# Three feed-forwards of a two-layer hybrid trunk: six leading weight tiles per half instead of four

## The reference, cut to what matters

```python
def swiglu(h, wg, wu, wd):
    return (jax.nn.silu(h @ wg) * (h @ wu)) @ wd

def sandwich_in(h, m, sub, p):
    return rms_norm(h, p['norm_pre'][sub]) * (1 + m[:, 3 * sub + 1]) + m[:, 3 * sub]

def sandwich_out(h, y, m, sub, p, weight):
    return h + weight * m[:, 3 * sub + 2] * rms_norm(y, p['norm_post'][sub])

def ffn_sub(h, m, sub, j, p):
    y = swiglu(sandwich_in(h, m, sub, p), p['w_gate'][j], p['w_up'][j], p['w_down'][j])
    return sandwich_out(h, y, m, sub, p, 0.5)

mod_x = (jax.nn.silu(c) @ w_mod[l] + b_mod[l]).reshape(bsz, N_MOD, 1, d)   # and mod_c from c_ctx
```

## Time and profile before

| | us |
|---|---|
| median of 3 runs | 2919.39 (2917.44 to 2920.51) |
| profiled execution | 2921.65 |
| its span, first to last instruction | 2919.8 |
| mean granted TensorE clock | 0.979 |

### The profile page before, as it was taken

One profiled execution on the slowest core, in us unless ns is written; L12 is line 12 of the kernel. 1 busy time (PEld: TensorE's weight loads), 2 busy tenths in 40 slices (PEclk: granted clock), 3 DMA queues, 4 the chain that ended last, 5 costly groups with the idle time before them and its releaser, 6 DMA issues.

```text
span 2919.8 us, 44695 instructions
## 1 busy us (share of the span) xinstructions
PE 2775.6 (95%) x17096; PEld 2649.4 (91%) x17096; DVE 2024.1 (69%) x3481; ACT 1095.6 (38%) x1888; POOL 805.3 (28%) x619
## 2 busy tenths in 40 slices
PE   6999999999999889999999899999999998899998
PEld 5999999988878889999999899999978877899997
DVE  4877889657345768989886789889656447664334
ACT  3312324453443452324245233324444534522233
POOL 2700313240043275312225821313240123400002
...
GB/s 231 136 154 134 128 130 94 144 149 56 89 55 33 109 152 76 128 137 91 136 100 144 134 113 102 131 129 87 152 133 58 127 36 81 133 144 89 93 93 111
DMA packets 468063, 332.24 MB, mean 114 GB/s; under 512 B 36118, under 2 KB 419452, under 8 KB 467340
## 3 DMA queue, kind: packets, MB, share of 16 engines
...
## 4 chain that ended last, share of the span: by engine, by line
PE 73%; DVE 12%; POOL 4%; ACT 4%; issue 4%; DMA 1%; SPq 0%; POOLq 0%; ACTq 0%; DVEq 0%
PE ps L2282 21%; PE ps L2284 21%; PE ps L2283 21%; POOL scr L842 3%; ACT wsp L1061 2%; DVE wsp L1581 2%; DVE macc L1624 2%; PE ps L2710 2%; PE ps L2685 1%; PE ps L2686 1%; DVE hn L1687 1%; POOL wsp L851 1%; ACT hn L1112 1%; PE ps L2697 1%; PE ps L2344 1%
## 5 line engine op out<-in xcount | busy, mean ns | idle before, releaser
L2282 PE MATMUL ps<-hn,wsp 128*128 128x384 f32 (+1 forms) x2400 | 785.7, 327 | 38.4 <-DVE hn L1687 19.3
L2283 PE MATMUL ps<-hn,wsp 128*128 128x384 f32 (+1 forms) x2400 | 776.3, 323 | 0.0
L2284 PE MATMUL ps<-hn,wsp 128*128 128x384 f32 (+1 forms) x2400 | 775.9, 323 | 0.0
L1581 DVE TENSOR_TENSOR wsp<-raw,wsp 128x1024 fp32r<-128x1024 f32 (+2 forms) x304 | 349.7, 1150 | 325.0 <-ACT wsp L1061 323.4
L2282 PEld LDWEIGHTS ps<-hn,wsp 128*128 128x128 f32 x2400 | 459.9, 192 | 56.8 <-issue 23.3
L1061 ACT ACTIVATE wsp<-raw 128x1024 fp32r<-128x1024 f32 (+2 forms) x344 | 324.9, 945 | 470.8 <-PE ps L2284 255.4
L2283 PEld LDWEIGHTS ps<-hn,wsp 128*128 128x128 f32 x2400 | 461.0, 192 | 0.0
L2284 PEld LDWEIGHTS ps<-hn,wsp 128*128 128x128 f32 x2400 | 460.4, 192 | 0.0
L2282 PE MATMUL ps<-aT,wsp 128*128 128x384 f32 (+1 forms) x1344 | 439.8, 327 | 16.6 <-DVE wsp L1581 5.6
L2284 PE MATMUL ps<-aT,wsp 128*128 128x384 f32 (+1 forms) x1344 | 433.7, 323 | 0.0
L2283 PE MATMUL ps<-aT,wsp 128*128 128x384 f32 (+1 forms) x1344 | 433.7, 323 | 0.0
(11 more groups left out here) (288 smaller groups left out, 4847.2 us busy)
## 6 DMA issues: line engine op xcount, KB each, us to landing
...
raw<-in_ffn_w_down SPq DMA_DIRECT2D x128, 192.0 KB, 2.8
...
```

The lines of the kernel that those rows point to most:

```text
L1581: dve.tensor_tensor(wsp[:, t % 2, 1, 0:width], raw[:, t % RAW, 0:width], wsp[:, t % 2, 0, 0:width].bitcast(F32), ALU.subtract).then_inc(wl ...
L2282: pe.matmul(dst, w(0), x(0), start=first, stop=False)
L2283: pe.matmul(dst, w(0), x(1), start=False, stop=False)
L2284: return pe.matmul(dst, w(1), x(0), start=False, stop=last)
```

## The change

In the three feed-forwards after the first:

- The lead has three chunks, six tiles, per half (`head_chunks`, `LONG_BANKS`): tiles 0 to 5 on half 0 and 6 to 11 on half 1. One whole chunk and the half chunk are left in group 0. Matmuls are as many as before; two more tiles are loaded and split in each.
- The mean for half 1 stands in the fifth tile, (4, 3), its spreading ahead of the sixth, (5, 0). GpSimd makes the low parts of tiles 2, 6 and 7 (before: 2 and 5).
- Tiles 4 and 5 take PSUM banks 1 and 3, so the scaled slices of half 1 go to SBUF, into `wsum` (`tmpS`, `scaled`).
- The splits of tiles 8 to 11 stand between the activations of the lead.
- Group 0's gate and up phase has no modulation; its eight pieces go to down tiles: in (0,1) and (1,0) four more in group 0's down phase, two each at the last down tile of groups 1 and 2; in (1,1) eight at down tiles 2 to 5 of group 0.

```diff
+def head_chunks(l, j): return 2 if (l, j) == (0, 0) else 3
+def up_tiles(l, j, g): return 9 - 2 * head_chunks(l, j) if g == 0 else 2 * GROUPS[g][1]
+def heads(l, sub): return HEAD if sub == 1 else 2 * head_chunks(l, sub // 2)
...
 HEAD_BANKS = [[0, 2, 4, 5], [6, 3, 0, 2]]
+LONG_BANKS = [[0, 2, 4, 5, 1, 3], [6, 7, 0, 2, 4, 5]]
...
-            if 0 <= i < HEAD:
-                return i in (0, 3) and (l, sub) != (0, 0)
+            if 0 <= i < heads(l, sub):
+                return i in ((0, 3) if heads(l, sub) == HEAD else (0, 4, 5)) and (l, sub) != (0, 0)
...
+LONG = {
...
+    "POOL": [("head", 0)] + [("xsq", 1, k) for k in PAIRS] + [("head", 4), ("head", 5)],
+    "PE": {(0, 5): ("mean", 1, 1), (0, 6): ("spread", 1, 1), (4, 3): ("mean", 0, 1), (5, 0): ("spread", 0, 1)},
+}
...
-    (1, 1): {(0, UP): [2, 2, 2, 2, 0, 0], (1, UP): [2, 2, 2, 2, 0, 0, 0, 0, 0, 0]},
+    (1, 1): {(0, DOWN): [0, 0, 2, 2, 2, 2, 0, 0], (1, UP): [2, 2, 2, 2, 0, 0, 0, 0, 0, 0]},
...
+            tmpS = wsum[:, 0:2, 0:HW]
...
+        def scaled(l, sub, n, k, a, b):
+            if n == 1 and heads(l, sub) > HEAD:
+                return tmpS[:, k % 2, a:b]
+            return tmp2[k % 2][:, a:b]
...
                 for n, (a, w) in enumerate(hv):
-                    for b in range(2):
-                        t = t0 + HEAD * n + 2 * b
-                        if n == 1:
+                    for b in range(hc):
+                        t = t0 + 2 * hc * n + 2 * b
+                        own = n == 1 and (b > 0 or hc == 2)
+                        if own:
                             next_lo(t)
-                        activated(q0 + 2 * n + b, b, b, a, w, HEAD_BANKS[n][2 * b + 1], units_before(t) + 2)
-                        if n == 1:
+                        activated(q0 + hc * n + b, (hc * n + b) % 2, b, a, w, head_banks(l, 2 * j)[n][2 * b + 1],
+                                  units_before(t) + 2)
+                        if own:
                             next_lo(t + 1)
+                        if n == 0 and hc > 2 and b != 1:
+                            next_lo(t0 + 2 * hc + b // 2)
...
-                for k in range(HEAD):
+                for k in range(heads(*cur)):
                     if k == 2 and cur != (0, 0):
                         pe.wait_ge(yadd_done, last_down0(*prev) + DOWN_OUT + 2)
+                    if k == HEAD:
+                        pe.wait_ge(x_done, KD * (post_event(*prev, 1) + 1))
...
-                for k in range(HEAD):
+                hc = head_chunks(l, j)
+                for k in range(2 * hc):
                     if k >= 2:
-                        pe.wait_ge(silu_done if k == 2 else amul_done, q0 + 3)
+                        pe.wait_ge(amul_done if k % 2 else silu_done, q0 + 2 + k // 2)
+                    elif k == 1 and hc > 2:
+                        pe.wait_ge(xr_done, KD * (pre_event(l, 2 * j, 1) + 1))
```

97 lines of the change are left out of this document (55 added, 42 removed).

## The result

| | us |
|---|---|
| before, median of 4 | 2919.95 (2917.44 to 2922.0) |
| changed kernel, median of 4 | 2954.32 (2946.32 to 2955.76) |
| ratio | 1.0112, 95% interval 1.0093 to 1.0132 |
| profiled execution, span | 2954.1, 2952.0 |

A forecast was written before the change was run, and what follows sets the result against it. TensorE, busy 95% of the span, loses time only to waits and half-clock stretches. 6.0 + 6.8 - 0.2 + 2.1 - 1.5 - 1.5 - 2.7 - 1.6 = 7.4 us less; median 2912 us, range 2902 to 2922.

The forecast's parts named there:

- what the lead is worth: Leads of (0,1), (1,0) and (1,1): the longer lead gains 6.0, 6.8 and -0.2 us.
- (a): Leads of (0,1), (1,0): spread's end to eighth low part takes 9.4 us, TensorE has 7.8 of work; 1.6 lost.
- (b): Same leads: with slices in SBUF, low parts contend with GpSimd's splits; doubling gives 2.3 us, holding 2.4; 2.4 taken.
- (c): Same leads: splits of tiles 8 to 11 hang on a ScalarE and VectorE chain beside GpSimd's sums; 2.9 us lost.
- (d): Same leads: one fall of the clock likely, most of it absorbed; 0.7 us lost (none to 5).
- (1,1) gains nothing: Lead of (1,1): new losses of 10.5 us against 10.3 before, so nothing gained.
- Reductions gone: Ahead of group 0's first result: the two reductions go with the modulation, gaining 0.6, 0.6 and 0.9 us, 2.1 together.
- Down phase of group 0: Modulation there overloads VectorE: 1.5 us lost in (0,1) and (1,0) each, 2.7 in (1,1); bounds 0 and 4.
- Last down tile of groups 1 and 2: Four modulations replace two reductions: uncontended no wait, with one slowed 0.8 us in each of two feed-forwards, 1.6 together.
- The slower one: Rival, 13%: groups 1 and 2's last-down-tile modulations meet GpSimd's weight sums, 15.8 us lost instead of 1.6; 2926.
- Clean: Rival, 17%: slices in SBUF cost nothing, down phases absorb the modulation; 2897 at the very end, 2904 with half.
- the wait moves: Rival, 20%: lead split chain loses 2.7 us more, clock stays half behind tile 9; 8.8 given back, 2921, no change.

The follow-up runs named there:

- two_steps_11: Changed kernel with loads and transposes moved and pieces two a step at places without cost, but (1,1)'s lead and pieces as before the change: 2919.1 us, ratio 0.9993.
- loads_turn: Changed kernel with last down tile's modulation loads behind the next group's first two tiles, transposes behind its fourth product: 2925.0 us, ratio 1.0021.

## Why the prediction was wrong

- **Bound, and what the lead is worth: right, with luck in the sum.** 6.0, 6.3 and 0.8 us gained against 6.0, 6.8 and -0.2. The terms inside missed in opposite directions: (a) and (b) together 4.0 predicted, the wait 2.9; (b) as held: 1.4 + 1.3 us for the 2.4 taken, and doubling would have given two slow low parts per pair; (c) 2.9 predicted, 1.0 seen in (0,1), at tile 9; (d) 0.7 predicted, but 0.89 over 32 us means 3.5 us lost to the clock.
- **(1,1) gains nothing: right**, shown by two_steps_11.
- **Reductions gone: right.** The wait for the first result of group 0's down phase (0.6 us in (0,1)) is absent from PE's rows of the changed kernel; it lies within D0, so what D0 lost is hidden in the table by as much.
- **Down phase of group 0: right mechanism named, mis-sized.** 1.5, 1.5 and 2.7 were predicted, 4.8, 3.1 and 5.6 measured. TensorE waited 0.4 us or less at each of the tiles named and up to 1.0 in (1,1). The sum counted VectorE's work against TensorE's and left out that weights land late (ScalarE's idle of 5.5 us ended by a transfer, VectorE's of 1.56, against 5.35 and 0.84 before), that the last pieces meet GpSimd's sums (4.81 us for four, 3.78 before, and a wait of 1.3 us at the end), and the clock: behind the wait for `aT` at the phase's start (1.8 us, before 1.1) it was 0.83 from 1136 to 1146 us in (0,1), 1.7 us lost, and 1.00 at the same place in (1,0). In (1,1), where there are no such sums, moving the pieces back brought 4.5 us, 0.8 of it transposes.

```profile
1174.70 4.81 DVE L1648 SCALAR_TENSOR_TENSOR macc<-modw,silc,macc 128x512 f32<-128x512 f32 x4
...
1174.75 3.78 DVE L1624 SCALAR_TENSOR_TENSOR macc<-modw,silc,macc 128x512 f32<-128x512 f32 x4
```

- **Last down tile of groups 1 and 2: this step failed.** "Four modulations replace two reductions ... uncontended 2.65, no wait", 1.6 us, became 32. I counted the seconds of VectorE between two of its instructions, and missed two queues: SyncE's, in which a modulation load waits for a buffer ahead of the next group's weights ("loads run two or three tiles ahead, nothing" was wrong at just this place), and TensorE's, in which a unit's transposes stand behind the last down tile as soon as the unit ends there. loads_turn gives back 24 of the 32 us (8.2 are left in its four stretches) without moving a piece. The sign of being wrong that I had named last, sevens' operands behind modulation, is the wait of 2.40 us.
- **The rivals.** The slower one named the place and gave 2926, but its mechanism (GpSimd's sums) is all but absent there: of the last tile's four one is slowed in the changed kernel (3.30 us in all) and none with the loads in time (2.72). What meets the sums then is the seventh tile's four (5.82), which stand in the kernel before as well. *Clean* fails by the two held pairs, *the wait moves* by the 1.0 us at tile 9.
